# Pieces of the shared expert's jobs between the last tile's stages, with transposed rows stored by the front

## The reference, cut to what matters

```
u   = rms_norm(x);  P = u @ w_in -> b, c, h (512 each), q (512), k, v (128 each)
y_conv = b * causal_conv3(c * h)
y_attn = sliding-window attention (window 128, 8 heads, 2 kv heads, ALiBi, sinks)
x   = x + concat(rms_norm(y_conv), rms_norm(y_attn)) @ w_out
xn  = rms_norm(x)
scores = sigmoid(xn @ w_router)          # 64 experts in 8 groups; top 4 groups, top 8 experts
routed = sum over 8 chosen experts of weight * swiglu_e(xn)     # width 256 inside
out = x + routed + swiglu_shared(xn)     # width 256 inside
```

## Time and profile before

| what | value |
|---|---|
| time, median of 3 runs (lowest to highest) | 1578.25 us (1576.15 to 1582.68) |
| the profiled execution's own time; its span | 1575.08 us; 1573.3 us |
| busy: TensorE, VectorE, ScalarE, GpSimd | 1493.4, 679.4, 294.9, 688.3 us |
| the chain that ended last | PE 94%, DVE, DMA, issue and ACT 1% each |
| front without the last tile | to 441.04 us |
| last tile, shared jobs | 441.04 to 603.83 us |
| routed jobs | from 604.78 us |
| SiLU and hidden product of a shared job | 0.38 and 0.66 us |

### The profile page before, as it was taken

One profiled execution on the slowest core, in us unless ns is written; L12 is line 12 of the kernel. 1 busy time (PEld: TensorE's weight loads), 2 busy tenths in 40 slices (PEclk: granted clock), 3 DMA queues, 4 the chain that ended last, 5 costly groups with the idle time before them and its releaser, 6 DMA issues.

```text
span 1573.3 us, 24266 instructions
## 1 busy us (share of the span) xinstructions
PE 1493.4 (95%) x6767; PEld 671.4 (43%) x6768; DVE 679.4 (43%) x892; ACT 294.9 (19%) x564; POOL 688.3 (44%) x639
## 2 busy tenths in 40 slices
PE   7999999999967999999999999999999999999990
PEld 3556656656643444333333333333333333333330
DVE  1434445444433424444444444444444444444440
ACT  1232332332330000111111111111111111111110
POOL 2010213213222201565655656656656556566562
PEclk9999999999977999999999999999999999999995
DMA  9310110110253524998999889888899989898825
GB/s 349 133 41 20 61 47 14 61 60 17 77 222 88 128 91 164 311 302 294 302 299 352 260 282 333 233 260 254 264 301 346 320 287 303 277 290 256 272 35 116
DMA packets 72042, 319.51 MB, mean 203 GB/s; under 512 B 14935, under 2 KB 16472, under 8 KB 46532
## 3 DMA queue, kind: packets, MB, share of 16 engines
q1 hardware_dynamic: 41764, 237.52, 41.6%
q0 software_dynamic: 30240, 81.50, 21.6%
HBM read 280.11 MB, written 60.89 MB: 217 GB/s over the span
## 4 chain that ended last, share of the span: by engine, by line
PE 94%; DVE 1%; DMA 1%; issue 1%; ACT 1%; POOL 0%; DVEq 0%; SPq 0%; POOLq 0%; ACTq 0%
PE psP L636 55%; PE psW L636 30%; PE psT L789 6%; PE psW L819 1%; PE psW L687 1%; DMA wts<-in_w_in_dram 1%; PE psT L723 0%; PE psT L644 0%; PE psT L709 0%; ACT area L962 0%; POOL out_dram L627 0%; PE psW L664 0%; DMA x_dram<-area,sidx 0%; DVE area L1258 0%; DVE st_s L1223 0%
## 5 line engine op out<-in xcount | busy, mean ns | idle before, releaser
L636 PE MATMUL psP<-wts,area 128*64 (+2 forms) x1344 | 571.5, 578 | 8.3 <-DMA wts<-in_w_in_dram 4.5
L636 PE MATMUL psW<-wts,area 128*64 128x512 f32 (+2 forms) x1592 | 429.5, 596 | 7.3 <-DVE wts L1490 3.7
L636 PEld LDWEIGHTS psP<-wts,area 128*128 128x128 f32 (+1 forms) x1344 | 216.5, 166 | 307.3 <-issue 298.2
L636 PE MATMUL psP<-wts,bias 128*64 (+1 forms) x688 | 305.2, 596 | 1.3 <-DVE bias L1386 1.3
L636 PE MATMUL psP<-area 128*64 128x512 f32 x640 | 283.2, 595 | 0.0
L636 PE MATMUL psP<-area,bias 128*64 128x512 f32 x624 | 276.1, 595 | 0.0
L636 PEld LDWEIGHTS psW<-wts,area 128*64 128x64 f32 (+1 forms) x1592 | 151.6, 148 | 259.1 <-issue 254.7
L597 POOL DMA_INDIRECT out_dram<-area,sidx x79 | 120.1, 1521 | 268.0 <-ACT area L1073 137.8
L578 POOL COPY gidx<-area 128x1 int32 (+1 forms) x83 | 202.7, 2442 | 69.0 <-PE psT L789 69.0
L1482 DVE COPY area<-wts 128x4096 f32 x81 | 186.1, 2297 | 94.9 <-issue 86.9
L597 POOL DMA_INDIRECT x_dram<-area,sidx x79 | 171.5, 2171 | 25.8 <-issue 23.9
(11 more groups left out here) (205 smaller groups left out, 955.8 us busy)
## 6 DMA issues: line engine op xcount, KB each, us to landing
wts<-in_w_exp_gate_dram SPq DMA_DIRECT2D x64, 1024.0 KB, 9.5
wts<-in_w_exp_up_dram SPq DMA_DIRECT2D x64, 1024.0 KB, 12.3
wts<-in_w_exp_down_dram SPq DMA_DIRECT2D x64, 1024.0 KB, 7.3
wts<-in_w_in_dram SPq DMA_DIRECT2D x4, 2048.0 KB, 17.7
area<-in_x_dram SPq DMA_DIRECT2D x8, 512.0 KB, 3.5
wts<-in_w_out_dram SPq DMA_DIRECT2D x1, 4096.0 KB, 19.5
area<-u_dram SPq DMA_DIRECT2D x16, 256.0 KB, 2.8
xn_dram<-area POOLq DMA_DIRECT2D x8, 512.0 KB, 3.0
```

The source lines that it names most:

```text
L636: return nc.tensor.matmul(out_, lhsT, rhs, start=start, stop=stop)
```

## The change

1. In the front, SyncE stores the transposed rows `xnT` of every tile into a new DRAM tensor (`store_xnT`), and `read_yT`, which overwrites that buffer, waits for the store of the tile before.
2. A shared job loads its transposed tile directly (`shared_xT`) into one of five places (`shared_place`): the first three over buffers of the front, the others in two halves of `bias`. `t_job` and `read_xT` are left to the routed jobs.
3. `front` stops one tile earlier. The last tile's stages are written out in each engine's program, with pieces of shared jobs 0 to 3 between them. `t_h` of a shared job writes to psP, not to psW; there are two `hT` buffers; `sg` and `hh` lie in `dsq`, not in `kv_sb`.
4. VectorE does `route` of tile 6 after `read_yT` of tile 7, not before it. ScalarE does SiLUs between the exponentials and the sigmoids.
5. The table transposes stand in the middle of gate_up(6); the first two gathered tiles are transposed after down(4) and down(5).

```diff
+        xnT_dram = nc.dram_tensor("xnT_dram", [S, D], F32).ap()
...
-        sg, hh = kv_sb[:, 0, :], kv_sb[:, 1, :]
+        sg, hh = dsq[:, 0:FE], dsq[:, FE:2 * FE]
+        xT = [bias[:, b * (NH // 2):(b + 1) * (NH // 2), :].rearrange("p h (a n) -> p (h a) n", n=P) for b in range(2)]
+        xT_early = [uT] + [area[:, o:o + D].rearrange("p (k n) -> p k n", k=KT) for o in (gates_at, gates_at + 2 * DC)]
...
-            for T in tiles:
+            for T in tiles[:-1]:
...
+        TB, TL = tiles[-2:]
+        def shared_place(j):
+            return (xT_early[j], r_ld[j], 1) if j < 3 else (xT[j % 2], r_ld[3 + j % 2], (j - 3) // 2 + 1)
...  SyncE
+            def store_xnT(T):
+                sp.wait_ge(s_xnT_ready, T.t + 1)
+                sp.dma_start(xnT_dram[T.rows, :], xnT.rearrange("p k n -> p (k n)")).then_inc(s_xnT_st, 16)
...
+                if B:
+                    store_xnT(B)
...
+            sp.wait_ge(s_xnT_st, 16 * (NT - 2))
             sp.wait_ge(s_proj, NT * NGR)
+            shared_xT(0)
             load_w(0, w_sh_gate[0], w_sh_up[0], w_sh_down[0])
+            sp.wait_ge(s_conv, 6 * NT)
+            sp.wait_ge(s_qk_norm, 8 * NT)
+            shared_xT(1)
+            shared_xT(2)
             load_w(1, w_exp_gate[0, 0], w_exp_up[0, 0], w_exp_down[0, 0])
             load_w(2, w_exp_gate[0, 1], w_exp_up[0, 1], w_exp_down[0, 1])
+            sp.wait_ge(s_soft, 5 * (NT - 1) + 1)
+            shared_xT(3)
+            shared_xT(4)
+            store_xnT(TB)
             sp.wait_ge(s_x1_ready, NT)
-            sp.wait_ge(s_xn_st, 16 * (NT - 1))
-            ...
             load_w(3, w_exp_gate[0, 2], w_exp_up[0, 2], w_exp_down[0, 2])
+            shared_out(0)
+            store_xnT(TL)
+            sp.wait_ge(s_xnT_st, 16 * NT)
+            for j in range(5, NSH):
+                sp.wait_ge(s_gu, j - 1)
+                shared_xT(j)
+                shared_out(j - 4)
...  GpSimd: rsqrt_xn(TB), store(TB), scatter_slots(5), rsqrt_ya(TL), rsqrt_xn(TL), store(TL), scatter_slots(6), (7)
...  TensorE, after front(step)
-            t_xn(TL)
-            router(TL)
-            ...
+            gate_up(0, range(0, 2))
+            scores(TL)
+            gate_up(0, range(2, KT))
+            t_xn(TB)
+            gate_up(1, range(0, 6))
+            t_p(TL, False)
+            gate_up(1, range(6, KT))
+            p_v(TL, False)
+            t_h(0, psP[:, 0, :])
+            router(TB)
+            t_h(1, psP[:, 1, :])
+            gate_up(2, range(0, 4))
+            t_y(TL)
+            gate_up(2, range(4, 6))
+            out_project(TL, 0)
+            position(TB)
+            out_project(TL, 1)
+            gate_up(2, range(6, KT))
+            pe.wait_ge(s_x1_ready, NT)
+            down(0)
+            gate_up(3, range(0, 2))
+            t_xn(TL)
+            gate_up(3, range(2, 4))
+            router(TL)
+            gate_up(3, range(4, KT))
+            down(1, (0,))
+            t_h(2, psP[:, 0, :])
+            position(TL)
+            down(1, (1,))
...  (count and job list matmuls, with gate_up(4) in two pieces between them)
+            t_h(3, psP[:, 1, :])
+            down(2)
+            gate_up(5)
+            t_h(4, psP[:, 0, :])
+            down(3)
+            gate_up(6, range(0, 4))
...  (wait s_jobs_ld, table transposes)
+            gate_up(6, range(4, KT))
+            t_h(5, psP[:, 1, :])
+            down(4)
+            t_job(NSH, 0, 1)
+            gate_up(7)
+            t_h(6, psP[:, 0, :])
+            down(5)
+            t_job(NSH + 1, 1, 1)
+            t_h(7, psP[:, 1, :])
+            down(6)
...  ScalarE, after front(step)
+            x1_square(TB)
+            exps(TL, False)
+            read_xn(TB)
+            read_p(TL, False)
+            act.wait_ge(s_tqk, NT)
+            silu(0, 0)
+            silu(1, 1)
+            read_h(0)
+            y_attn_square(TL)
+            read_h(1)
+            y_attn_scale(TL)
+            sigmoid(TB)
+            x1_square(TL)
+            silu(2, 0)
+            read_xn(TL)
+            sigmoid(TL)
...  VectorE: in read_yT, and after front(step)
+                    dve.wait_ge(s_xnT_st, T.t * 16)
...
+            x1_add(TB)
+            xn_make(TB)
+            soft_a(TL, False)
+            soft_b(TL, False)
+            h_mul(0, 0, one_col[:, 0:1])
+            o_norm(TL)
+            h_mul(1, 1, one_col[:, 0:1])
+            y_attn_rms(TL)
+            read_yT(TL)
+            route(TB)
+            read_pos(TB)
+            slots(TB)
             x1_add(TL)
             xn_make(TL)
+            h_mul(2, 0, one_col[:, 0:1])
+            read_shared(0, 0)
             route(TL)
             read_pos(TL)
             slots(TL)
```

More of the change, by code:

```diff
@@ L286, in hymba_moe @@
         g_ld = [sem(f"g_ld{b}") for b in range(2)]
-        r_ld = [sem(f"r_ld{b}") for b in range(2)]
+        r_ld = [sem(f"xT_ld{b}") for b in range(5)]
         sh_st = [sem(f"sh_st{b}") for b in range(2)]
@@ L560, in _ @@
             front(step)
-            rsqrt_xn(tiles[-1])
-            store(tiles[-1])
+            rsqrt_xn(TB)
+            store(TB)
+            scatter_slots(NT - 3)
+            rsqrt_ya(TL)
+            rsqrt_xn(TL)
+            store(TL)
             scatter_slots(NT - 2)
@@ L575, in gather @@
             def gather(j, par, copies):
-                pool.wait_ge(s_xg_t, j - 1)
+                if not isinstance(j, int) or j >= NSH + 2:
+                    pool.wait_ge(s_xg_t, j - (NSH + 1))
                 nc.gpsimd.tensor_copy(gidx[:, par:par + 1], tab_i[:, bass.ds(j - NSH, 1)]).then_inc(s_idx_cp, 1)
@@ L781, in step, with t_job @@
                 out_project(T, 1)
[L783 to L787, removed]
+            def t_job(j, par, nth):
+                pe.wait_ge(g_ld[par], nth * 16)
+                if not (isinstance(j, int) and j == NSH):
+                    pe.wait_ge(s_xT_ready, j - NSH)
                 for k in range(KT):
@@ L872, in _ @@
                 .then_inc(s_post_pe, 1)
-            gate_up(1, 1, range(4, 6))
+            gate_up(4, range(4, KT))
             pe.wait_ge(s_post, 6)
@@ L877, in _ @@
             mm(psW[0:JMAX, 1, 258:260], ended[:, JT:JT + JMAX], nb2[:, :], True, True).then_inc(s_post_pe, 1)
[L878 to L897, removed]
-                    for n, (j0, c) in enumerate(((0, 0), (0, 1), (HB, 0))):
-                        i = nc.tensor.transpose(psW[:, 1, n * P:(n + 1) * P], tabT[:, j0:j0 + P, c], ident[:, :])
-                    i.then_inc(s_tab_t, 1)
-                t_h(j)
+            t_h(3, psP[:, 1, :])
[4 more added lines that the diff above has]
+            gate_up(6, range(0, 4))
+            pe.wait_ge(s_jobs_ld, 32)
+            pe.wait_ge(s_post_pe, 6)
+            pe.wait_ge(s_jobrow, 4)
+            for n, (j0, c) in enumerate(((0, 0), (0, 1), (HB, 0))):
+                i = nc.tensor.transpose(psW[:, 1, n * P:(n + 1) * P], tabT[:, j0:j0 + P, c], ident[:, :])
+            i.then_inc(s_tab_t, 1)
+            gate_up(6, range(4, KT))
[8 more added lines that the diff above has]
+            down(6)
             pe.wait_ge(s_n_jobs, 4)
@@ L1047, in _ @@
             front(step)
-            TL = tiles[-1]
-            x1_square(TL)
-            read_xn(TL)
-            sigmoid(TL)
             def silu(j, par):
@@ L1060, in read_h @@
                 act.wait_ge(s_th, j + 1)
-                if not (isinstance(j, int) and j == 0):
+                if isinstance(j, int) and j < NSH:
+                    if j >= 2:
+                        act.wait_ge(s_down, j - 1)
+                    A(hT[(j + 1) % 2].rearrange("p f n -> p (f n)"), psP[:, j % 2, 0:FE], ACT.Copy).then_inc(s_hT_ready, 1)
+                else:
                     act.wait_ge(s_down, j)
-                A(hT.rearrange("p f n -> p (f n)"), psW[:, 0, 0:FE], ACT.Copy).then_inc(s_hT_ready, 1)
+                    A(hT[0].rearrange("p f n -> p (f n)"), psW[:, 0, 0:FE], ACT.Copy).then_inc(s_hT_ready, 1)
             def read_y(j, par, static):
@@ L1382, in read_xT @@
             def read_xT(j, par):
-                dve.wait_ge(s_xg_t, j + 1)
-                if not (isinstance(j, int) and j < 2):
-                    dve.wait_ge(s_gu, j - 1)
+                dve.wait_ge(s_xg_t, j - (NSH - 1))
+                dve.wait_ge(s_gu, j - 1)
                 V.tensor_copy(xT[par], psT[:, :, :]).then_inc(s_xT_ready, 1)
```

194 lines of the change are left out of this document (90 added, 104 removed).

## The result

| | before | changed |
|---|---|---|
| median of 4 runs, us | 1578.43 (1576.15 to 1582.68) | 1542.76 (1541.63 to 1544.1) |
| profiled execution's span, us | 1573.3 | 1538.9 |
| end of TensorE's work on tile 6 to first routed matmul, us | 441.04 to 604.78: 163.7 | 442.88 to 570.74: 127.9 |
| first routed matmul to the end of the span, us | 968.5 | 968.2 |

The ratio is 0.9771, 95% interval 0.9749 to 0.9794. The change saves 36 us where 50 were forecast, and the time lies 2.8 us above the range. The last row says where to look: all of the gain and all of the shortfall lie ahead of the routed jobs.

What follows compares the result with a forecast made beforehand. TensorE bounds the routed jobs; ahead of them the last tile's four-engine chain leaves it idle. The profiled 1575.1 less 52.1 saved plus 3 of stalls gives 1526.0; 2 more for the median gives 1528 us, range 1521 to 1540.

Steps and rivals of the forecast that it cites:

- The sum of the work: From TensorE's end on tile 6 to its last shared work: 110.7 us at full clock against 162.8, saving 52.1.
- the covers for softmax, route, the output addition and the two last normalized rows: Last tile's stretch: shared-job pieces fill TensorE's waits for these stages, leaving none except 0.2 us at the last route.
- The store of tile 6's transposed rows: Issued at 456.6, needed by read_yT at 470: no wait if it takes 4.5 us, 5 us if 18.3.
- Stalls taken: New waits in the stretch: 0.3 + 0.2 + 0.4 and 2 us for handovers and queues: 3 us, ends 0 and 9.
- rival (b): A late transfer for shared tile 5, read_yT or the job table makes TensorE wait: 13 us, 1538; chance 0.18.
- Tile 5: Shared tile's load behind a store and its wait, needed at 515: there by 505, or at worst a 2.1 us wait.
- Job table: After the last scatters: ready at 525, TensorE at its table transposes at about 529, slack 4 us.
- Probability copy: ScalarE's copy of the last tile's probabilities takes 1.89 us, two k-steps cover 1.72: a wait of 0.3.
- Front stores: A 512 KB store per front step, awaited by read_yT: 20 us of cover for a 4.5 us transfer, cost nil.
- (d): Slower: the new store holds up read_yT in each of seven tiles, time over 1586 us; chance 0.03.
- (c): Gain given back in the routed jobs, where expert weights bound the loop: 1575 to 1578 us; chance 0.04.
- Table loads: ScalarE in the stretch: six in place of three, 1.28 us each or 2.66 with a drain; at most 0.1 wait.

Runs made afterwards that it cites:

- The kernel with late scatters, early places and a late table: Changed kernel with tile 5's scatters after rsqrt_ya, shared tiles 5, 6, 7 in the places of tiles 1, 2, 0, table transposes after down(4): 1526.66 us.
- repeat: The changed kernel measured and profiled once more with no edit: 1542.44 us, ratio 0.978 to the kernel before.

## Why the prediction was wrong

**The sum of the work was right.** It gave 110.7 us of work and 3 of stalls, 113.7, first routed matmul at about 555. The kernel with late scatters, early places and a late table has 441.10 to 555.22, 114.1 us, at clock 1.00: 112.45 of them busy, with modelled ends, and 1.67 idle. That confirms the order's columns, the 52 us, and the covers for softmax, route, the output addition and the two last normalized rows, none of which has a hole over 0.32 us there; the last 1.10, at the first routed matmul, answers to the 0.95 of the earlier trace rows. The forecast was made for a kernel whose transfers are in time, and the changed kernel isn't that one.

**The step that failed** is "The store of tile 6's transposed rows, on which read_yT waits ... 4.5 gives no wait, 18.3 gives 5", and with it "Stalls taken", 3 us with an upper end of 9. The store took 22.25 us, over both ends. The hole ahead of the output projection is 7.0 to 8.6 us (8.60, 7.01, 7.43) in three of the five profiles with unchanged scatters, with half clock around it; in the other two, 1.72 and 3.67, TensorE had lost 1.80 before P times V already. Moving the scatters away from it gave 10.4. I had named the scatters as evidence for rival (b), but priced the store by the landings of SyncE's loads, and read the longest, 18.3, as "behind weights". It was more than that. In the kernel before, this load is issued at 506.45, and POOL issues the scatters of tile 6 from 499.69 to 508.64. SyncE's queue from 494 to 500, and from 504 to 508:

```profile
q1 hardware_dynamic: 288, 1.05, 46.9%
```

```profile
q1 hardware_dynamic: 44, 0.36, 111.0%
```

That is 0.16 us a packet (46.9% of 96 us, by 288) and 1.6 beside the scatters (111.0% of 64, by 44; these are 8 KB, of weights, which from 442 to 450 take 0.29). So the 18.3 already held the collision, with the weights ahead of it in the queue slowed too, and it was no upper end for a store whose neighbours are scatters. The timeline of before also had the place: its scatters of route(5) are issued from 448.37 to 457.34, and the new store was to come at 456.6.

**Two other margins** were spent in the same way. Tile 5: its store and load together were given 9.0 us, and 22.8 at worst; they took 24.7 (505.04 to 529.7) and, with late scatters, 25.7 (14.38 and 11.34). The hole was 1.7 to 4.3 in place of at most 2.1. Job table: 5 us from the last scatter to the read-back, measured 12.3 to 16.1; slack 4, hole up to 5.0 where the earlier ones had not covered it. They were taken one at a time, and one hides the other: mending tile 5 alone gained nothing, mending both but not the table gained no more than the scatters did.

**Rival (b) is what happened**, with its three places (read_yT, tile 5, table) and its form (wait, then half clock). It gave 13 us in place of 3 and 1538; measured by stretch 127.9 (first profile) and 130.9 (repeat, 441.80 to 572.68), so 17 to 20 over the work in place of 3. Between the repeat and the kernel with the late table and early places, 130.9 less 114.1 are 16.8: 8.60 + 1.74 + 1.90 + 1.14 = 13.4 of holes, and 4.6 us at half clock after 481.34, which lose 2.3; 1.1 is not assigned. I should have given (b) more than 0.18: three new waits on transfers in a stretch with 24 scatters of small packets are not three independent margins. That the time missed the range by only 2.8 us is no merit of the stalls term, which was 14 to 17 us short.

**The rest.** Probability copy: 0.3 expected, 0.25 found, save for two profiled kernels with 1.80, where ScalarE's copy began late (461.45, behind transposes that had started at 457.96); not explained. Front stores: nil, as said (ratio 1.0001), so (d) falls; the 1.8 us by which the first profile of the changed kernel starts its stretch later are not theirs, as the repeat and others start it at 440.9 to 441.8 with the same stores. Routed jobs: 968.2 for 968.5 us, so (c) falls. Table loads: at the second of its six in the stretch the changed kernel's ScalarE has

```profile
461.45 1.88 ACT L1014 ACTIVATE area<-psW 128x2048 f32<-128x2048 f32 x1 [3.08 <-remote]
463.35 1.28 ACT L1090 ACT_TABLE_LOAD   x1
464.64 0.38 ACT L1090 ACTIVATE dsq<-psP 128x256 f32<-128x256 f32 x1
```

1.28 us and the SiLU directly behind it. The Trainium skill (ScalarE: Activation LUTs, "What ACT_TABLE_LOAD costs") counts 2.66 with a drain; in three of the six the next function starts within 0.02 us, which leaves no place for one (behind the other three ScalarE was idle for 1.1 to 6.5 us, so they can't tell). TensorE waited for none of the six.

## What to carry to other kernels

Before a transfer is put under a wait, list what every queue issues around it, small indirect scatters above all: price it by the landing in that company, not by the median of its own kind. Where one landing is far above the others, look up what ran beside it before taking it as a bound. Where several transfers have thin margins in one stretch, mend all, since each earlier hole hides the later. Here it was enough to move the small scatters or the asking instruction by one product, without touching the transfer.

## What the runs showed of the hardware

- A 512 KB store or load of 4 KB packets and the slot table's scatters slow each other. SyncE's packets, 0.16 us without, took 0.76 to 0.99 us (means over 24 and 8 us), those of the scatters 0.11 in place of 0.015; the store landed after 22 us in place of 4 to 7, the read-back could start 12.3 to 16.1 after the last scatter's issue ended, in place of 5.0 and 6.0. The DMA share read 0.96 from 466 to 474 meanwhile, at 54 GB/s.
- The Trainium skill (DMA: Bandwidth & Descriptors, "Queues, rings and completion order") says that an engine takes turns between its queues, packet by packet. Such turns would let a 4 KB packet wait; the rows show that its recorded time grows five- to sixfold. Whether that time includes such waiting, and whether the small size of the scatters' pieces, their indirect addresses or the second queue is what matters, no run here tells.
- Every hole of TensorE of 2.28 us and more in the stretch of the changed kernels came with half clock: 10.2 us of it at those of 8.60 (from 475.7) and 7.43, 6.8 at 7.01 and around the table holes of 4.7 to 5.0, 3.4 at the 3.22, 4.31, 2.28 and 2.83 of tile 5 and at the 3.67. It can begin inside the hole. Of shorter ones, 1.72, 1.74, 1.90, 1.14 and 1.10 had none. The same 1.80 before P times V had 10.2 us of it from 465.6 on in the first profile, and none in the kernel with the late table alone, where P times V took 3.79 in place of 5.10; so the length of the hole alone does not settle it.
